# A hybrid block on one core: every tile of 1 KB or more moved to a multiple of 256 bytes

## The reference

```
x  = x + sum_n sigmoid(h @ w_merge_gate[n]) * (y_n @ w_branch[n]) @ w_out
h2 = rms_norm(x)
x  = x + sum over 2 chosen experts e of  w_e * (silu(h2 @ w_g[e]) * (h2 @ w_u[e])) @ w_d[e]
```

## Time and profile before

| | us |
|---|---|
| median of three runs | 711.92 |
| the profiled execution's own time | 712.9 |
| its span, first to last instruction | 711.1 |
| TensorE busy in the span | 587.2 |
| VectorE busy | 302.8 |
| ScalarE busy | 189.7 |

### The profile page before, as it was taken

One profiled execution on the slowest core, in us unless ns is written; L12 is line 12 of the kernel. 1 busy time (PEld: TensorE's weight loads), 2 busy tenths in 40 slices (PEclk: granted clock), 3 DMA queues, 4 the chain that ended last, 5 costly groups with the idle time before them and its releaser, 6 DMA issues.

```text
span 711.1 us, 15452 instructions
## 1 busy us (share of the span) xinstructions
PE 587.2 (83%) x6636; PEld 410.9 (58%) x6636; DVE 302.8 (43%) x626; ACT 189.7 (27%) x332; POOL 29.6 (4%) x56
## 2 busy tenths in 40 slices
PE   8999999999999999996875767776678656887584
PEld 5787899999999885553432333333334333443342
DVE  6475976985474945442222222122312222111412
ACT  4493355473535434110111001010011100110111
POOL 8003000000000020000000000000000000000000
PEclk9999999999999999998798788797877988687969
DMA  8995546536579699999999999999999999999993
GB/s 253 349 328 187 163 137 203 175 121 213 175 274 420 234 395 369 427 425 428 425 427 425 426 429 427 426 427 427 425 425 428 427 427 427 424 426 427 423 417 146
DMA packets 39619, 247.73 MB, mean 348 GB/s; under 512 B 4360, under 2 KB 6496, under 8 KB 25472
## 3 DMA queue, kind: packets, MB, share of 16 engines
q1 hardware_dynamic: 38096, 245.44, 85.6%
q0 software_dynamic: 912, 1.25, 1.0%
q10 hardware_dynamic: 544, 0.06, 0.1%
HBM read 245.67 MB, written 1.06 MB: 347 GB/s over the span
## 4 chain that ended last, share of the span: by engine, by line
PE 50%; DMA 44%; SPq 1%; another core or an unknown queue 1%; DVE 1%; issue 1%; ACT 0%; ACTq 0%; DVEq 0%
DMA wide<-in_w_expert_up 38%; PE ps L1366 8%; PE ps L1029 6%; PE ps L1030 6%; PE ps L1031 6%; DMA wide<-in_w_expert_down 3%; PE ps L1401 3%; PE ps L1002 3%; PE ps L1004 3%; PE ps L1003 3%; PE ps L1325 2%; DMA ring<-in_w_in 2%; PE ps L1413 1%; PE ps L1381 1%; SPq L526 1%
## 5 line engine op out<-in xcount | busy, mean ns | idle before, releaser
L1366 PE MATMUL ps<-wide,xe 128*32 128x256 f32 x2048 | 162.1, 470 | 109.3 <-DMA wide<-in_w_expert_up 109.3
L1366 PEld LDWEIGHTS ps<-wide,xe 128*32 128x32 f32 x2048 | 75.9, 131 | 176.9 <-issue 132.1
L1882 DVE TENSOR_TENSOR xe<-ps,g_ffn 128x256 f32<-128x256 f32 x32 | 13.6, 425 | 258.4 <-PE ps L1334 258.4
L1486 DVE TENSOR_TENSOR ring_lo<-ring,w_hi 128x1024 fp32r<-128x1024 f32 x76 | 92.0, 1228 | 46.2 <-ACT w_hi L721 45.7
L721 ACT ACTIVATE w_hi<-ring 128x1024 fp32r<-128x1024 f32 x76 | 79.0, 1058 | 58.8 <-PE ps L1031 35.3
L1029 PE MATMUL ps<-hT_hi,w_hi 128*128 128x256 f32 x320 | 89.4, 279 | 0.2 <-DVE hT_lo L1498 0.2
L1030 PE MATMUL ps<-hT_lo,w_hi 128*128 128x256 f32 x320 | 88.4, 276 | 0.0
L1031 PE MATMUL ps<-hT_hi,ring_lo 128*128 128x256 f32 x320 | 88.4, 276 | 0.0
L925 ACT ACTIVATE he<-ps 128x128 f32<-128x128 f32 x32 | 8.9, 278 | 207.7 <-PE ps L1381 204.7
L1401 PE MATMUL ps<-wide,he 128*32 128x256 f32 x1024 | 62.5, 382 | 1.9 <-DMA wide<-in_w_expert_down 1.8
L1029 PEld LDWEIGHTS ps<-hT_hi,w_hi 128*128 128x128 f32 x320 | 60.1, 188 | 0.7 <-issue 0.7
(11 more groups left out here) (276 smaller groups left out, 785.9 us busy)
## 6 DMA issues: line engine op xcount, KB each, us to landing
wide<-in_w_expert_gate SPq DMA_DIRECT2D x27, 2048.0 KB, 45.6
wide<-in_w_expert_up SPq DMA_DIRECT2D x27, 2048.0 KB, 48.2
wide<-in_w_expert_down SPq DMA_DIRECT2D x27, 2048.0 KB, 41.1
ring<-in_w_in SPq DMA_DIRECT2D x8, 2048.0 KB, 16.1
ring<-in_w_merge_gate SPq DMA_DIRECT2D x6, 2048.0 KB, 9.6
wide<-in_w_expert_gate SPq DMA_DIRECT2D x10, 1024.0 KB, 13.2
wide<-in_w_expert_up SPq DMA_DIRECT2D x10, 1024.0 KB, 10.6
wide<-in_w_expert_down SPq DMA_DIRECT2D x9, 1024.0 KB, 11.8
```

Source lines behind the costliest of these rows:

```text
L1366: ins = t_.matmul(ps[q * WIN:(q + 1) * WIN, b, 0:QW], xe[b][:, k % 2, k // 2, :], w, start=(k == 0), stop=(k == KD - 1))
L1486: v.tensor_tensor(piece(ring_lo, g, c), piece(ring, g, c), by_row(out_hi[g == 19][c]).bitcast(F32), ALU.subtract).then_inc(wpre_lo, 1)
```

## The change

The first offset becomes 16,640 instead of 16,512. `fitting` rounds an offset up to a multiple of 256 for a tile of 1,024 bytes or more and of 64 for a smaller one; `place` and `here` use it. Every offset that is kept for a later tile (`w_hi_at`, `x_at`, `reset_at` and the others) is rounded the same way, so that tiles that lie over others begin at such multiples too. No instruction, wait or DMA differs otherwise.

```diff
-    top = [16512]
+    top = [16640]
+
+    def fitting(at, size):
+
+        step = 256 if size >= 1024 else 64
+        return (at + step - 1) // step * step
 
     def place(name, shape, dt, at=None):
         size = int(np.prod(shape[1:])) * mybir.dt.size(dt)
-        off = top[0] if at is None else at
+        off = fitting(top[0], size) if at is None else at
         if at is None:
-            top[0] = off + (size + 31) // 32 * 32
+            top[0] = off + size
...
-        w_hi_at = top[0]
+        w_hi_at = top[0] = fitting(top[0], 1024)
...
-        region = top[0]
+        region = fitting(top[0], 1024)
 
         def here(name, shape, dt):
-            nonlocal_at = here_at[0]
-            here_at[0] += (int(np.prod(shape[1:])) * mybir.dt.size(dt) + 31) // 32 * 32
-            return place(name, shape, dt, at=nonlocal_at)
+            size = int(np.prod(shape[1:])) * mybir.dt.size(dt)
+            off = fitting(here_at[0], size)
+            here_at[0] = off + size
+            return place(name, shape, dt, at=off)
...
-        sig0_at = here_at[0]
+        sig0_at = here_at[0] = fitting(here_at[0], 1024)
...
-        aqk_at = here_at[0]
+        aqk_at = here_at[0] = fitting(here_at[0], 1024)
```

More of the change, by code:

```diff
@@ L133, in hybrid_block @@
             top[0] += 4 * SLOT
-        w_hi_at = top[0]
+        w_hi_at = top[0] = fitting(top[0], 1024)
         w_hi = [place(f"w_hi{c}", [P, CW], F32R) for c in range(CHUNKS)]
-        x_at = top[0]
+        x_at = top[0] = fitting(top[0], 1024)
         x_tok = place("x_tok", [P, TT, D], F32)
-        xn_at = top[0]
+        xn_at = top[0] = fitting(top[0], 1024)
         xn = place("xn_merged", [P, TT, D], F32)
@@ L153, in hybrid_block @@
         on_w = place("on_w", [P, 1], F32)
-        w_al_at = top[0]
+        w_al_at = top[0] = fitting(top[0], 1024)
         w_al = place("w_al", [16, 256], F32)
@@ L159, in hybrid_block @@
         table = place("table", [BUCKETS, NH], F32)
-        w_z_at = top[0]
+        w_z_at = top[0] = fitting(top[0], 1024)
         w_z = place("w_z", [P, KD, 16], F32)
@@ L167, in hybrid_block @@
         stat = place("stat", [P, 64], F32)
-        reset_at = top[0]
+        reset_at = top[0] = fitting(top[0], 1024)
         reset = place("reset", [P, T], F32)
@@ L181, in hybrid_block @@
         rt = place("rt", [P, TT, 16], F32)
-        other_at = top[0]
+        other_at = top[0] = fitting(top[0], 1024)
         other = place("other", [P, TT, NE], F32)
@@ L209, in hybrid_block @@
         bias_row = place("bias_row", [NH, 384], F32, at=region + 4 * T)
-        yc_at = here_at[0]
+        yc_at = here_at[0] = fitting(here_at[0], 1024)
         ycT = here("ycT", [P, KC, T], F32)
@@ L213, in hybrid_block @@
         conv_u = here("conv_u", [P, KC, T + 2], F32)
-        hT_at = here_at[0]
+        hT_at = here_at[0] = fitting(here_at[0], 1024)
         hT_hi = here("hT_hi", [P, KD, T], F32R)
-        h2T_at = here_at[0]
+        h2T_at = here_at[0] = fitting(here_at[0], 1024)
         hT_lo = here("hT_lo", [P, KD, T], F32R)
@@ L220, in hybrid_block @@
         merged_hi = place("merged_hi", [P, KD, T], F32R, at=hT_at)
-        aqk_at = here_at[0]
+        aqk_at = here_at[0] = fitting(here_at[0], 1024)
         aqk = here("aqk", [P, 2, TT, C], F32)
-        q_at = here_at[0]
+        q_at = here_at[0] = fitting(here_at[0], 1024)
         qTz = here("qTz", [P, NH, T], F32)
@@ L228, in hybrid_block @@
         gqk = here("gqk", [P, 4, T], F32)
-        att_at = here_at[0]
+        att_at = here_at[0] = fitting(here_at[0], 1024)
         attm = here("attm", [P, 8, P], F32)
-        gv_at = here_at[0]
+        gv_at = here_at[0] = fitting(here_at[0], 1024)
         out_hi = [w_hi, [place(f"out_hi{c}", [P, CW], F32R, at=gv_at + 4 * CW * c) for c in range(CHUNKS)]]
         gv = here("gv", [P, TT, C], F32)
-        gr_at = here_at[0]
+        gr_at = here_at[0] = fitting(here_at[0], 1024)
         gr = here("gr", [P, TT, C], F32)
         kdn = here("kdn", [P, TT, 256], F32)
-        sbd_at = here_at[0]
+        sbd_at = here_at[0] = fitting(here_at[0], 1024)
         sbd = here("sbd", [P, 3, 2, 256], F32)
-        scr_at = here_at[0]
+        scr_at = here_at[0] = fitting(here_at[0], 1024)
         scr = here("scr", [P, 2, C], F32)
```

## The result

The changed kernel takes 714.80 us, the median of six runs (713.78 to 718.61), against 711.92 (711.28 to 713.08) of the kernel before beside it: a ratio of 1.0040, 95% interval 1.0025 to 1.0055. That is outside the predicted range of 707.9 to 713.9, and more than the 0.2% that the prediction counted as no change. So the two traces side by side show 0.9 us of loss where the medians show 2.9.

The account below looks back on a forecast made before the run. The prediction took matmul cadence from 26 to about 252 us, then the rate of weight rows, as the bound. Its terms 0 + 0 + 0 left the median at 711.9 us, with a range of 707.9 to 713.9.

Parts of the forecast that it names:

- What bounds the kernel: Whole kernel: matmul cadence sets the time from 26 to about 252 us, the rate of weight rows after that.
- (a) VectorE and ScalarE = 0: VectorE and ScalarE operations: tile offsets change at most 2 ns in 420, taken as 0.
- (b) TensorE = 0: TensorE matmuls: a 3.8% slower cadence comes and goes at the same addresses, so the change was taken as 0.
- this rival: Slow cadence spreads: equal offsets could put 1,104 more matmuls into it, 4.6 us slower, to 716.5; chance 0.11.
- (c) DMA rows = 0: Weight loads: full slices stay at 423 to 429 GB/s at differing offsets, so taken as 0, bounds 5.8 us either way.
- the rival near the truth: DMA row starts cost the bytes below them to a multiple of 256: 3.7 us faster, to 708.2; chance 0.16.
- The bound of 6.1 ns a row: DMA loads: the most a shifted start can save per row beside its bytes, 5.8 us in all.
- The sum: Whole kernel: 0 + 0 + 0, profiled execution stays at 712.9 us and median at 711.9; no change 0.71.
- the two rivals: Dearer DMA row starts removed, 3.7 us faster, chance 0.16; slow TensorE cadence spreading, 4.6 us slower, chance 0.11.

Follow-up runs that it names:

- e2: Changed kernel with every large tile 64 bytes further, all at 64 instead of 0 modulo 256; 718.40 us, ratio 1.0080.
- e12: Changed kernel with every slot, weight and branch tile at 128 and hT alone at 64; 714.74 us in a single run.
- e4: Changed kernel with ring slots, w_hi, x_tok and xn at 128 as before, second region at 0; 716.43 us, ratio 1.0060.
- e5: Changed kernel with hT_hi and hT_lo alone at 192 modulo 256; 710.96 us, ratio 0.9983.
- e6: Changed kernel with hT_hi, hT_lo and the branch outputs (ycT, yc, ya, yg) at 192; 708.60 us, ratio 0.9945.
- e8: Changed kernel with weights and ring slots at 64, the second region at 0; 711.35 us in a single run.
- e1: Changed kernel with hT_hi and hT_lo alone back at 64 modulo 256; 714.01 us, ratio 1.0017.
- e3: Changed kernel with ring slots, w_hi, x_tok and xn at 0, the second region at 64; 714.85 us, ratio 1.0031.

## Why the prediction was wrong, by its own steps

**What bounds the kernel** held: the matmul cadence to about 252 us, the rate of rows after that. Both effects reached the time, each in its half.

**(a) VectorE and ScalarE = 0** held. Busy 302.7 and 189.5 us. The groups by line and shape in after, beside the earlier trace rows:

```profile
L744 ACT ACTIVATE gv<-ps 128x512 f32<-128x512 f32 x2 | 1.1, 586 | 0.0
L744 ACT ACTIVATE ycT<-ps 128x512 f32<-128x512 f32 x2 | 1.1, 586 | 0.0
L1785 DVE CUSTOM_DVE_ANT_0 xn<-x_tok 128x256 f32<-128x256 f32 x2 | 0.8, 424 | 0.1
L1785 DVE CUSTOM_DVE_ANT_0 junk<-x_tok 128x256 f32<-128x256 f32 x2 | 0.8, 424 | 0.1
```

**(b) TensorE = 0 is the step that failed.** It read rightly from the earlier trace rows that one tile runs at two speeds at the same address, and concluded that "the offsets alone do not fix it". What followed from the rows is only that a fixed offset does not forbid a slow group; whether another offset forbids the fast ones was never in them, since all weights were at 128 and the slow and the fast hT tokens at 64. What the runs show in its place is the difference of the two operands: 113 ns at 64, 120 at 0, worth 6.0 to 6.8 us by the square. The change, by making all offsets equal, set it to 0 everywhere. The chance of 0.11 for this rival was too low for a change whose one sure effect is to make all offsets equal, which that rival named as its trigger.

The rival's size was short as well. It took all matmuls at the 118 ns of yc, 3.8%, and got 4.6 us; they went to 120, which no row of before showed. In its own sum that is 1,104 x 6.7 ns + 144 x 2.2 ns = 7.7 us. The table of starts has 6.7 of them from 93 us on; 0.6 us belong to the 96 of them that run before 23 us, where weights are waited for anyway, and 0.4 stay unaccounted for. The 240 matmuls of 128x512, all before 93 us, became a little faster (229.1 to 227.5 ns, 0.4 us).

**(c) DMA rows = 0 failed too, with the rival near the truth.** That rival had 428.5 GB/s or more and 3.7 us; measured were 429 GB/s, and 3.1 to 3.9 us by the square. The bound of 6.1 ns a row was itself a slip: it took a KB as 1,000 bytes for the slope and as 1,024 for the row. With 1,024 in both, 80.7 and 615.4 ns give 38.2 ns per KB and 4.3 ns a row, so 4.1 us instead of 5.8. That smaller bound held too: the mean of the 16 KB rows fell by 3.7 ns. The rates where rows are 2 and 8 KB did not rise: 404 GB/s (199 to 201 us) and 420 (211 to 231 us) in after, against 406 and 421. The rival's mechanism, a price in proportion to the bytes below the start, did not hold: e2 (64 everywhere) and e12 (128 everywhere) are both at 426, and e4, with seven slots at 128, reaches 428. The step leaned on flat slices at offsets of 128, 64 and 32, and all of those are slow: none was at 0, which the prediction called its weak point. The durations of single 16 KB rows in the traces, 10,421 in each, in ns:

```
                     shortest common   at it        mean
before (128/64/32)   611               2,885 rows   619.7
e2  (all at 64)      611               1,089 rows   619.9
e12 (all at 128)     611               3,338 rows   619.7
e4  (4 of 11 at 0)   611               8,479 rows   617.3
after (all at 0)     611              10,197 rows   616.0
```

Rows of 611 ns occur at every offset. What the alignment removes is the spread just above it (6,791 rows of 612 to 620 ns before, 66 after), not one fixed price on every row. The Trainium skill's rule ("DMA: Bandwidth & Descriptors", "How a descriptor splits into AXI transactions"), which the prediction set against its own zero, speaks of bytes that are fetched; read for the side written to, the only one that changed here, it has the direction right and comes near the size: an estimate of 0.8% from that page for a row at 128, against 0.7% measured for the mix of 128, 64 and 32. By that rule a row at 64 should cost half of what one at 128 does in excess beats; e2 against e12 shows no such step (426 GB/s in both), so the measurement decides against reading it as beats per row.

**The sum.** 0 + 0 + 0 took the two rivals as alternatives, each with a chance of its own. They act on different halves and don't exclude each other, and both happened: the case "both", 4.6 - 3.7 = +0.9 by the prediction's own sizes, got no chance at all. By those sizes both would still have ended inside the range, at 712.8; what carried the median 0.9 us past its end at 713.9 is the cadence term of (b), 6.0 to 6.8 us instead of 4.6. That zero came within 0.4% all the same is luck: two wrong zeros of opposite sign nearly cancel.

**What stays open.** Why the difference matters to TensorE is not shown; that the moving data gets into the way of the next weights is a guess that no run tests, and `w_hi` and `ring_lo` had the same offset in every kernel, so which of them counts is open too. So is what sets the cadence of a single group after a pause: 118 ns at a difference of 64 in before, e5, e6, e8 and e12, 113 at 192 in e1. Why a ring with only some slots at 0 does nearly as well as one with all was not settled by e3, e4 and e8. Differences of 224, and steps finer than 32, were not run.

## What to carry to other kernels

Align the tiles that DMA streams into to 256 bytes where the loads are the bound, but do not take it that matmul operands want one alignment as well: here the 128x256 matmuls ran best with the weights 64 bytes (modulo 256) above the moving tokens, the 128x512 ones with both at the same offset. That is a thing to try out in a few layouts, not to assume. Before giving two opposite mechanisms separate chances, ask whether they exclude each other; if they sit in different stages, the sum of both is a case of its own. When a property of one operand seems not to matter because it is the same in fast and slow rows, look for the relation between operands that the rows never varied.

## What was not expected of the hardware

- The start-to-start time of 128x256 matmuls with 128x128 weights, both in SBUF, depends on the relative offset of weights and moving data: 113.3 ns at 64 (modulo 256), 117.6 to 120 ns on the mean at the six other differences tried, at the same granted clock of 1.00. The three pairs 128/64, 0/192 and 64/0 were alike. Single groups after a pause ran at 117.8 at 64, and one at 113.3 at 192.
- Where the tokens are held and the weights move, in 128x512 matmuls, the order is another: 227.5 ns at 0, 229.1 to 229.6 at 64, 232.5 to 234.2 at the others.
- A sequence in which one matmul of three has a slow difference runs most of the way at the slow cadence (118.3 ns, between 113.3 and 120, where own prices would give 115.6).
- Loads of 16 KB rows reach 429 GB/s where every slot begins at a multiple of 256 bytes, 426 where all begin at 64 or all at 128; single rows of 611 ns occur in all three.
- The kernel of e6, all large tiles at multiples of 256 but for the moving ones at 192, takes 708.6 us: 0.55% less than the kernel before (interval 0.37% to 0.74%), and 0.9% less than the change as made (708.6/714.8, medians of different runs, so without an interval).
